# A two-layer hybrid flow trunk on one core: the norm chain between producer and joint products is rebuilt, and conditioning work is moved

## The reference

```
h  = RMSNorm(x) * (1 + sc1) + sh1            # norm 1, adaLN
three mixers of h, gates, branch products -> merged
x  = x + g1 * (merged @ w_out)               # OUT
h2 = RMSNorm(x) * (1 + sc2) + sh2            # norm 2, adaLN
up = dwconv3(h2 @ ffn_w_up)                  # UP
x  = x + g2 * ((silu(up_gate) * up_val) @ ffn_w_down)   # DOWN
final: RMSNorm(x)
RMSNorm(x) = x * rsqrt(mean(x*x) + eps) * g
```

## Time and profile before

| what | us |
|---|---|
| median of 3 runs | 1434.77 (1432.1 to 1435.72) |
| profiled execution | 1430.01 |
| its span | 1428.2 |
| PE busy, share | 1343.2, 94% |
| DVE busy, share | 1064.3, 75% |
| ACT busy, share | 650.4, 46% |
| mean granted clock of PE | 0.970 |

### The profile page before, as it was taken

One profiled execution on the slowest core, in us unless ns is written; L12 is line 12 of the kernel. 1 busy time (PEld: TensorE's weight loads), 2 busy tenths in 40 slices (PEclk: granted clock), 3 DMA queues, 4 the chain that ended last, 5 costly groups with the idle time before them and its releaser, 6 DMA issues.

```text
span 1428.2 us, 19924 instructions
## 1 busy us (share of the span) xinstructions
PE 1343.2 (94%) x7558; PEld 1280.2 (90%) x7558; DVE 1064.3 (75%) x1884; ACT 650.4 (46%) x1031; POOL 155.7 (11%) x179
## 2 busy tenths in 40 slices
PE   6899999999997999999979998999999799999995
PEld 4799788899996999999969987898999799999995
DVE  5889887578856999999967787627886588888332
ACT  4543444544546444542355334545444655445231
POOL 0056000000310000000111800000031100000001
PEclk8899999999998999999989999999999899999998
DMA  9356424432333455557744561332234245444441
GB/s 366 133 197 218 154 88 169 150 102 89 118 119 103 162 170 170 171 176 253 258 133 133 191 222 59 104 103 89 89 104 132 89 158 158 141 149 135 127 122 45
DMA packets 58287, 208.94 MB, mean 146 GB/s; under 512 B 6736, under 2 KB 8912, under 8 KB 56784
## 3 DMA queue, kind: packets, MB, share of 16 engines
q1 hardware_dynamic: 55648, 197.53, 42.0%
q0 software_dynamic: 2544, 10.14, 2.1%
HBM read 203.97 MB, written 3.68 MB: 145 GB/s over the span
## 4 chain that ended last, share of the span: by engine, by line
PE 66%; DVE 21%; ACT 6%; issue 5%; DMA 1%; POOL 1%; SPq 0%; ACTq 0%; DVEq 0%
PE acc L800 20%; PE acc L802 19%; PE acc L801 19%; DVE wl L1442 5%; DVE junk_ffn L1496 3%; DVE junk_front L1496 1%; DVE gates L1607 1%; ACT cv L1160 1%; PE mix L944 1%; PE mix L1039 1%; ACT wh L1121 1%; DMA head<-in_whead_dram 1%; PE mix L972 1%; DVE cv L1568 1%; DVE cv L1570 1%
## 5 line engine op out<-in xcount | busy, mean ns | idle before, releaser
L800 PE MATMUL acc<-hh,wh 128*128 128x386 f32 x1600 | 561.7, 351 | 25.4 <-DVE hl L1447 20.1
L802 PE MATMUL acc<-hh,wl 128*128 128x386 f32 x1600 | 549.1, 343 | 0.0
L801 PE MATMUL acc<-hl,wh 128*128 128x386 f32 x1600 | 548.8, 343 | 0.0
L1442 DVE TENSOR_TENSOR wl<-raw,wh 128x1024 fp32r<-128x1024 f32 (+1 forms) x280 | 344.1, 1229 | 159.2 <-ACT wh L1121 157.1
L1121 ACT ACTIVATE wh<-raw 128x1024 fp32r<-128x1024 f32 (+1 forms) x280 | 291.1, 1041 | 137.9 <-PE acc L802 137.7
L800 PEld LDWEIGHTS acc<-hh,wh 128*128 128x128 f32 x1600 | 306.6, 192 | 42.9 <-issue 28.6
L801 PEld LDWEIGHTS acc<-hl,wh 128*128 128x128 f32 x1600 | 307.9, 192 | 2.7
L802 PEld LDWEIGHTS acc<-hh,wl 128*128 128x128 f32 x1600 | 307.0, 192 | 0.0
L800 PE MATMUL acc<-ah,wh 128*128 128x386 f32 x352 | 119.3, 339 | 0.0
L801 PE MATMUL acc<-al,wh 128*128 128x386 f32 x352 | 119.2, 339 | 0.0
L802 PE MATMUL acc<-ah,wl 128*128 128x386 f32 x352 | 119.1, 338 | 0.0
(11 more groups left out here) (242 smaller groups left out, 1572.0 us busy)
## 6 DMA issues: line engine op xcount, KB each, us to landing
raw<-in_wstream_dram SPq DMA_DIRECT2D x248, 512.0 KB, 3.5
rawm<-in_wstream_dram SPq DMA_DIRECT2D x80, 512.0 KB, 3.8
raw<-in_wstream_dram SPq DMA_DIRECT2D x32, 448.0 KB, 3.3
head<-in_whead_dram SPq DMA_DIRECT2D x8, 1024.0 KB, 13.9
crow<-in_cvec_rows_dram POOLq DMA_DIRECT2D x2, 1024.0 KB, 7.4
out_y_dram<-gates POOLq DMA_DIRECT2D x8, 193.0 KB, 2.8
prm<-in_par_dram POOLq DMA_DIRECT2D x2, 591.5 KB, 4.7
x<-in_xs_dram SPq DMA_DIRECT2D x1, 1024.0 KB, 7.8
```

What stands on the lines that cost most here:

```text
L800: mm(out, sh, mhi, start=start, stop=False)
L801: mm(out, sh, mlo, start=False, stop=False)
L802: return mm(out, sl, mhi, start=False, stop=stop)
L1442: tt(wl[:, s, 0:n], raw[:, raw_slot(u), 0:n], wh[:, s, 0:n].bitcast(F32), ALU.subtract).then_inc(lo_done, 1)
```

## The change

- `mean_squares` on PE now adds three products in PSUM: the sum of tiles 0 to 5 from POOL, the square of tile 6 (ACT) and that of tile 7, which DVE makes itself directly behind its update, ahead of the next `lo`. POOL leaves tiles 6 and 7 out.
- Tiles 0 and 1 of a norm are multiplied by their scale by ACT while OUT or DOWN still runs (`prescale`, behind OUT 2 and DOWN 6). Behind the norm, DVE multiplies by rs, ACT writes x·scale·rs + shift straight to `hh`, and DVE makes `hl` from both (two instructions, one per token group).
- The norm's buffers are four (`cv` and `th`), not two.
- `joint` runs wh·hh and wl·hh of three units behind the high part, then wh·hl of three units behind the low part, for tiles 0 to 5.
- The tanh table is loaded behind each norm. `row_tanh` and `rows_silu` move from behind norm 2 to UP unit 3, with one half of `junk` for each row.
- Mod tiles of layer 0 stand behind UP units 4, 7, ..., 43 and DOWN units 0 to 17. The four taken from DOWN 18 to 21 go to layer 1, where 16 stand behind units 8 to 23 (`FRONT`).
- POOL's cache load of layer 1 waits for the last mod tile of layer 0.

```diff
+POOLED_SQ = KT - 2
+ROWS_FFN = UP0 + JOINT
-    units += [(0, UP0 + 3 * i + 2) for i in range(14)] + [(0, DOWN0 + i) for i in range(22)]
-    units += [(1, MIX0 - 12 + i) for i in range(12)] + [(1, UP0 + 5 * i + 4) for i in range(MODT - MOD_G2)]
+    units += [(0, UP0 + 3 * i + 4) for i in range(14)] + [(0, DOWN0 + i) for i in range(18)]
+    units += [(1, u) for u in FRONT] + [(1, UP0 + 5 * i + 4) for i in range(MODT - MOD_G2)]
+        ring = [cv[:, 0, :], cv[:, 1, :], th[:, 0, :], th[:, 1, :]]
@@ POOL @@
-                    group_done(pool, l - 1, G_OF[(OUT, KT - 1)])
+                    pool.wait_ge(mod_used, sum(lu[0] < l for lu in MODS))
@@ PE, mean_squares @@
-                mm(mz, ones, sqa[:, :], start=True, stop=True).then_inc(misc_done, 1)
+                pe.wait_ge(sq_sum, POOLED_SQ * (n + 1))
+                mm(mz, ones, sqa[:, :], start=True, stop=False)
+                pe.wait_ge(sq_done, KT + (KT - 1) * (n + 1))
+                mm(mz, ones, th[:, (KT - 2) % 2, :], start=False, stop=False)
+                pe.wait_ge(sq_last, n + 1)
+                mm(mz, ones, th[:, (KT - 1) % 2, :], start=False, stop=True).then_inc(misc_done, 1)
@@ PE, joint @@
                 for k in range(KT - 2):
...
+                    pe.wait_ge(h_hi, count(l, NSPLIT, split0 + k))
+                    for i in range(JOINT):
+                        w1, w2 = weights(i, k)
+                        mm(banks[i][:, 0:T], w1, hh[:, k, :], start=(k == 0), stop=False)
+                        mm(banks[i][:, 0:T], w2, hh[:, k, :], start=False, stop=False)
                     pe.wait_ge(h_lo, count(l, NSPLIT, split0 + k))
                     for i in range(JOINT):
-                        product(i, k)
+                        mm(banks[i][:, 0:T], weights(i, k)[0], hl[:, k, :], start=False, stop=False)
@@ ACT @@
+            def prescale(l, nth):
+                scale = sc2 if nth else sc1
...
+                af(hh[:, 0:2, LAT:CTX0], x[:, 0:2, LAT:CTX0], ACT.Copy)
+                for j in range(2):
+                    for v, (a0, a1) in enumerate(SEGS):
+                        last = af(ring[j][:, a0:a1], x[:, j, a0:a1], ACT.Identity, scale=scale[:, j, v:v + 1])
+                    last.then_inc(prescaled, 1)
+            def norm(l, nth):
...
+                    if j < 2:
+                        for v, (a0, a1) in enumerate(SEGS):
+                            last = af(hh[:, j, a0:a1], b[:, a0:a1], ACT.Identity, bias=mod[:, shift0 + j, v:v + 1])
+                        last.then_inc(h_hi, 1)
                     else:
+                        affine(b, scale, shift0, j)
+                        high(l, None, hh[:, j, :], b)
+                act.preload_act_table_set(TANH_EXP)
-                    if v:
-                        act.wait_ge(crow_ready, 2 * n + v)
-                    af(junk[:, 0, :], rows[:, v, :], ACT.Tanh, scale=0.5).then_inc(crow_tanh, 1)
+                    af(junk[:, v, :], rows[:, v, :], ACT.Tanh, scale=0.5).then_inc(crow_tanh, 1)
+                    if u == ROWS_FFN:
                         row_tanh(l + 2, crow, junk_ffn)
@@ DVE, norm @@
+                    if j < 2:
+                        dve.wait_ge(prescaled, 2 * norm_number(l, nth) + j + 1)
+                        tt(ring[j], ring[j], rs[:, :], ALU.mult).then_inc(h_full, 1)
+                        return
+                    if j >= 4:
+                        dve.wait_ge(h_lo, count(l, NSPLIT, split0 + j - 4))
+                    tt(ring[j % 4], x[:, j, :], rs[:, :], ALU.mult).then_inc(h_full, 1)
...
+                for j in range(2, KT):
+                    full(j)
+                    low_tile(j - 2)
@@ DVE, update @@
+                if j == KT - 1:
+                    dve.wait_ge(sq_sum, POOLED_SQ * (n + 1))
+                    dve.wait_ge(x_new, KT * (n + 1))
+                    tt(th[:, j % 2, :], x[:, j, :], x[:, j, :], ALU.mult).then_inc(sq_last, 1)
@@ DVE, main loop @@
-                        rows_silu(l + 2, crow, junk_ffn)
+                    if u == ROWS_FFN:
+                        rows_silu(l + 2, crow, junk_ffn)
                     modulation(l, u)
```

More of the change, by code:

```diff
@@ L210, in scan_task, with norm_number @@
     return y_ if rest == 0 and 0 <= y_ < NY else None
+def norm_number(l, nth):
+    return 2 * l + nth - 1
 def count(l, per, i):
@@ L449, in build @@
         sq_sum = sem("sq_sum")
+        sq_last = sem("sq_last")
+        prescaled = sem("prescaled")
         rs_ready = sem("rs_ready")
@@ L876, in joint, with weights @@
                     banks.append(acc[g % BANKS])
+                def weights(i, k):
+                    s = (l * NU + u0 + i) % NHL
+                    return wh[:, s, P * k:P * k + P], wl[:, s, P * k:P * k + P]
                 def product(i, k):
-                    s = (l * NU + u0 + i) % NHL
-                    return three(banks[i][:, 0:T], wh[:, s, P * k:P * k + P], wl[:, s, P * k:P * k + P], hh[:, k, :],
-                                 hl[:, k, :], k == 0, k == KT - 1)
+                    w1, w2 = weights(i, k)
+                    return three(banks[i][:, 0:T], w1, w2, hh[:, k, :], hl[:, k, :], k == 0, k == KT - 1)
                 for k in range(KT - 2):
@@ L1102, in _ @@
                         mixers(l, u - MIX0)
-            misc_turn(DEPTH, 0)
-            pe.wait_ge(sq_sum, KT * 2 * DEPTH)
-            mm(mz, ones, sqa[:, :], start=True, stop=True).then_inc(misc_done, 1)
+            mean_squares(DEPTH, 0)
         @block.scalar
@@ L1144, in ahead, with affine, first_norm @@
                     hi(n // NU, n % NU)
-            def norm(l, nth, split0, scale, shift0):
+            def affine(b, scale, shift0, j):
+                for v, (a0, a1) in enumerate(SEGS):
+                    last = af(b[:, a0:a1], b[:, a0:a1], ACT.Identity, bias=mod[:, shift0 + j, v:v + 1],
+                              scale=scale[:, j, v:v + 1])
+                step.then(last)
+            def first_norm():
                 for j in range(KT):
                     b = cv[:, j % 2, :]
+                    act.wait_ge(h_full, F_N1 + j + 1)
+                    if j % 2 == 0 and 2 <= j <= KT - 4:
+                        shift_part(j // 2 + 1)
+                    act.wait_ge(scale_ready, j // 2 + 1)
+                    affine(b, sc1, 0, j)
+                    high(0, None, hh[:, j, :], b)
@@ L1151, in norm @@
+            def norm(l, nth):
+                scale, shift0 = (sc2, 3 * KT) if nth else (sc1, 0)
+                for j in range(KT):
+                    b = ring[j % 4]
                     act.wait_ge(h_full, count(l, NFULL, (F_N2 if nth else F_N1) + j))
-                    if l == 0 and nth == 0:
-                        if j % 2 == 0 and 2 <= j <= KT - 4:
-                            shift_part(j // 2 + 1)
-                        act.wait_ge(scale_ready, j // 2 + 1)
-                    else:
-                        act.wait_ge(scale_ready, KT // 2 + 2 * l + nth)
@@ L1159, in norm @@
-                    for v, (a0, a1) in enumerate(SEGS):
-                        last = af(b[:, a0:a1], b[:, a0:a1], ACT.Identity, bias=mod[:, shift0 + j, v:v + 1],
-                                  scale=scale[:, j, v:v + 1])
-                    step.then(last)
-                    high(l, None, hh[:, j, :], b)
+                    if j < 2:
+                        for v, (a0, a1) in enumerate(SEGS):
+                            last = af(hh[:, j, a0:a1], b[:, a0:a1], ACT.Identity, bias=mod[:, shift0 + j, v:v + 1])
+                        last.then_inc(h_hi, 1)
+                    else:
+                        affine(b, scale, shift0, j)
+                        high(l, None, hh[:, j, :], b)
@@ L1404, in _ @@
                         if kind in (OUT, DOWN):
-                            first = KT * (2 * l + (kind == DOWN))
-                            square(first, j, first + j)
+                            if j < KT - 1:
+                                square(2 * l + (kind == DOWN), j)
+                            if (kind, j) == (OUT, 2):
+                                prescale(l, 1)
+                            if (kind, j) == (DOWN, KT - 2) and l + 1 < DEPTH:
+                                prescale(l + 1, 0)
                         if kind == BRANCH and j >= 2 * KT:
@@ L1627, in update @@
                 last.then_inc(x_new, 1)
+                n = 2 * l + (kind == DOWN)
+                if j == 2 and n + 1 < 2 * DEPTH:
+                    nc.vector.tensor_copy(hl[:, 0:2, LAT:CTX0], x[:, 0:2, LAT:CTX0])
+                if j == KT - 1:
+                    dve.wait_ge(sq_sum, POOLED_SQ * (n + 1))
+                    dve.wait_ge(x_new, KT * (n + 1))
+                    tt(th[:, j % 2, :], x[:, j, :], x[:, j, :], ALU.mult).then_inc(sq_last, 1)
             def softmax_max(l, i):
```

70 lines of the change are left out of this document (44 added, 26 removed).

## The result

The changed kernel takes 1416.9 us (median of 4 runs, 1414.4 to 1420.1) beside 1433.4 for the kernel before on the same chip (4 runs): ratio 0.990, 95% interval 0.988 to 0.992. On another chip, in a later series, it took 1415.0 beside 1429.2, ratio 0.9895 (0.9877 to 0.9913). The profiled execution went from 1430.0 to 1417.9, by 12.1; the forecast was 1417.1, by 12.9. So the size is right from profile to profile. The forecast for the median was 1421.9, and 1416.9 came: inside the stated 1414.5 to 1429.5, but outside the forecast's own 1418.5 to 1425.5, because it was set 4.8 above the profiled execution, as in the kernel before, and here the profiled execution lies 1.0 above the median. The parts are right less often than the size: errors of 1 to 2.5 us in both directions cancelled.

A forecast was written before the change was run, and what follows sets the result against it. PE runs at its own pace nearly everywhere and loses at the norms. Terms -15.4 - 1.3 - 0.3 + 2.3 + 0.6 + 1.2 = -12.9 us: profiled 1430.0 to 1417.1, median 1421.9; range 1414.5 to 1429.5, the forecast's own 1418.5 to 1425.5.

The forecast's parts named there:

- The gap: At each norm, last product of OUT or DOWN to the joint's first product: 8.79 us becomes 5.2.
- The middle norm's condition: Norm 1 of layer 1: DVE is caught up without DOWN's last four mod tiles; if not, up to 2.7 us return.
- The joints: Joint behind each norm: 14.1 us, with 13.5 and 15.0 as ends, against 14.7, 14.3 and 15.25 before.
- The first joint: First joint of layer 0: high-half products start sooner but its end hangs on the last low part; -0.3 (0 to -1.2).
- The c rows: Rows moved from behind norm 2 to UP unit 3: +0.6 us in layer 0, +2.3 in layer 1.
- The rival that the rows would hide: UP, both layers: ACT and DVE catch up ahead of unit 7; -19.8 us in all, 1415.0; chance 18%.
- DOWN unit 21: Layer 0: UP's later mod tiles leave DVE less slack entering DOWN; nothing lost, at worst 1 us.
- VV of layer 1: Four more mod tiles in layer 1's FRONT bring a wait at the first VV unit: +1.2 us (0 to 2.7).
- the end: Behind the last product: square by DVE and 0.89 instead of ACT, POOL and 1.20; -1.3 us.
- the clock takes it back: Rival, 22%: joints stay 14.8, slow third product, a stall in each UP drops the clock; -6.2 us, 1428.6.
- its slow third product: Part of the clock rival: third product with ones at the norms stays slow, +0.5 us each, 1.6 in all.

The follow-up runs named there:

- the first profile: The changed kernel as described, profiled beside the kernel before: 1416.9 us, ratio 0.990; profiled execution 1417.9.
- the second: The changed kernel again, no edit, profiled in a later series on another chip: 1415.0 us, ratio 0.9895 to the kernel before.

## Why the prediction was right, and where it was not

**The gap, right.** 5.2 was built from single rows and came out as 5.17, 5.16, 5.17. The experiments split the 3.6 that one gap gained: undoing the sums alone gives back 1.8 to 2.5, the prescale 0.8, the product order 0.8. The middle norm's condition held too: without DOWN's last four mod tiles DVE is caught up, and with them the wait grows by 3.3 us and the gap by 4.0, where the bound was 2.7.

**The joints: half a chance, from a window that closed too soon.** The prediction took 14.1, half way between 13.5 (clock kept) and 14.7. Measured were 14.5 three times, 1.2 too little in the sum. The half rested on the earlier trace rows, of which the prediction read that an idle time of 2.51 kept clock 1.00. But that window ends at 180.00, 2.2 us behind the wait. These are the 14 us behind the same three waits of the kernel before (2.51, 1.99 and 1.99):

```profile
177.81:192.00 14.19, 13.14 (x73) 10.81 (x74) 12.72 (x37) 4.55 (x14) 0.00 (x0) 0.88 0.21 70
256.80:271.00 14.20, 14.20 (x83) 13.32 (x84) 7.00 (x11) 7.10 (x13) 0.00 (x0) 1.00 0.46 159
943.80:958.00 14.20, 14.20 (x75) 13.40 (x75) 1.23 (x1) 5.68 (x11) 0.00 (x0) 0.88 0.23 75
```

The clock fell behind two of the three, the longest among them, and it was low in all three joints of the earlier trace rows. So this step failed in its reading and not by bad luck: the trace of before spoke for joints near 14.7, which would have put the sum at -11.1. Over all kernels with 2.75 us of idle time and no longer wait just before it, 20 joints, 17 took 14.5 at 0.88, one 15.5 at 0.82, and 2 ran at 1.00 and took 13.3. The lower end of 13.5 was 0.2 too high.

**The first joint, a mis-sized term.** The step that failed: "its end hangs on the last low part, whose chain is untouched". The chain was not untouched, since it goes through PE. Between tiles of this joint PE makes the modulation's shift sums, ACT copies their parts, DVE turns them into the shifts, and ACT needs these for the next tiles. High-half products that start sooner let PE reach the shift sums sooner (41.28 instead of 45.21), and so the last low part comes sooner (50.22 instead of 52.55). -0.3 was predicted (0 to -1.2), -2.75 measured, and the old product order alone gives back 2.9.

**The c rows, right in size, wrong in what they were measured against.** +0.6 and +2.3 became +0.8 and +2.6, with the wait at unit 7 as forecast (1.80). At unit 8 nothing was left, for the slow clock behind the wait took its place; where the clock kept 1.00, in four such stretches of the experiments, unit 8 waited 0.68 or 0.69. But the prediction had the rows at the old place "hold up the weights of UP unit 3" and took all of that as belonging to the place. With two halves of the buffer the old place costs PE 0.4 per layer at unit 3, and the rest of the price belonged, by DVE's rows above, to the one half. The rival that the rows would hide was wrong about ACT and DVE catching up in UP, where nothing is free (9.5 of 10).

**The late rows, a missed term.** The buffer's halves serve a third place, the late stage, whose silu stands ahead of a softmax: -1.2, shown by restoring one half.

**DOWN unit 21, a mis-sized term.** Taken as 0, at worst 1; 1.14 of wait and 0.3 behind it in the first profile, 0.55 of wait in the second. ACT stands 3.19 in the parameter step for a DVE operation behind the last mod tile, and its weights come late. With the step two units later the wait is gone, in all three kernels that have it there.

**VV of layer 1 and the end, right**: a wait of 1.20 with 0.2 behind it, and 1.1, predicted 1.2 and 1.3.

**The mixers of layer 1, not part of the change.** Of their +1.2, 0.8 stands in the 25 us around attention, which no kernel here changes. Over the 14 us behind its 2.5 us wait the granted clock was 0.88 in the profile before and 0.65 in that of the changed kernel, and in all profiles this stretch took between 23.7 and 25.8.

Of the rivals, "the clock takes it back" got its joints and the fallen clock behind both stalls in UP. Only, that fall cost 0.1 us in layer 0 and 0.6 in layer 1, by the kernels in which the clock stayed up, and not 1.5 at each, for it stood in the place of a wait at unit 8; and its slow third product did not come (0.92 measured). That the sum came within 0.8 all the same is luck: errors in opposite senses (-2.5 and -1.2 on one side; +1.2, +1.4 and +1.2 on the other) cancelled.

## What to carry to other kernels

Before moving work away from a stall, ask whether its place or its form makes the stall: here a second half of a buffer did most of it, and the move cost 6 us, because it went from a stretch with idle engines to one without. A chain that ends in another engine's part can still run through the engine whose order is changed, so follow it to its start before calling it untouched. And two fixes at neighbouring places don't add up: the one lets the work arrive sooner at the other's limit. And a window that is to show what the clock did behind a stall has to run on well past the restart: here the fall came up to 2.2 us after it.
